# Mixture of experts in two blocks: an eighth home for expert matrices where x lies, loads in one piece, and a router that streams rows

## The reference

```python
# block one
x = x + diff_attention(rmsnorm(x), ...)            # 8 heads, two softmaxes each, causal
xt = rmsnorm(x, norm_ffn)                          # 512 x 1024
logit_g = xt @ w_group + b_group                   # 4 groups
logit_e = xt @ w_router + b_router                 # 4 experts in each
g = argmax(logit_g); two best experts e of group g, with weights w
y[n] = sum over the 2 experts of w * (silu(xt @ w_gate[e]) * (xt @ w_up[e])) @ w_down[e]
x = x + y
# block two
n = rmsnorm(x) * (1 + scale) + shift
p = n @ w_in                                       # Fourier input and gate, q, k, v, gate
x = x + gate * (concat(fourier(...), neighbourhood_attention(q, k, v, ctx)) @ w_out)
```

## Time and profile before

| | us |
|---|---|
| median of three timed runs | 907.3 (907.12 to 907.95) |
| the profiled execution | 915.63 |
| its span | 913.9 |
| PE busy in the span | 885.8 |
| mean granted TensorE clock | 0.988 of full |

### The profile page before, as it was taken

The page is one execution under the profiler, slowest core; times in us unless marked ns, Lnnn a source line. Parts: engine busy times, 40 slices in busy tenths (PEclk is TensorE's granted clock), DMA queues, the critical chain, the costliest instruction groups (busy, mean ns, idle before and its releaser), DMA issues.

```text
span 913.9 us, 13488 instructions
## 1 busy us (share of the span) xinstructions
PE 885.8 (97%) x5418; PEld 527.4 (58%) x5418; DVE 365.6 (40%) x824; ACT 210.7 (23%) x464; POOL 156.5 (17%) x155
## 2 busy tenths in 40 slices
PE   8999999999999999999898989899999999999998
PEld 5588875456564743345333333344688888856653
DVE  2765442457755473120202010047635542444331
ACT  2211223345543310110000000024202111633320
POOL 3211220000002052050302000033202213260000
PEclk9999999999999799999999999999999999999999
DMA  9945569124012978999999999961382102700002
GB/s 325 319 112 185 185 214 392 63 97 180 1 47 91 184 239 276 358 409 419 413 420 415 419 418 422 403 248 47 111 172 99 48 8 81 241 1 1 1 12 80
DMA packets 79455, 186.38 MB, mean 204 GB/s; under 512 B 32016, under 2 KB 32672, under 8 KB 68512
## 3 DMA queue, kind: packets, MB, share of 16 engines
q1 hardware_dynamic: 71072, 162.41, 49.5%
q0 software_dynamic: 4976, 16.79, 4.9%
q10 hardware_dynamic: 3344, 6.30, 1.8%
HBM read 168.17 MB, written 17.31 MB: 203 GB/s over the span
## 4 chain that ended last, share of the span: by engine, by line
PE 86%; DVE 4%; issue 3%; DMA 2%; ACT 2%; POOL 2%; SPq 0%; DVEq 0%; ACTq 0%; POOLq 0%
PE psum L1029 20%; PE psum L1241 17%; PE psum L1267 8%; PE psum L943 6%; PE psum L1408 5%; PE psum L1131 5%; PE psum L1079 4%; PE psum L1056 4%; PE psum L1093 2%; PE psum L1110 2%; PE psum L1479 2%; PE psum L1369 2%; PE psum L1153 1%; POOL qk_st L2708 1%; PE psum L992 1%
## 5 line engine op out<-in xcount | busy, mean ns | idle before, releaser
L1241 PE MATMUL psum<-ring,buf_a 128*32 128x512 f32 x1232 | 157.9, 597 | 3.1 <-issue 3.0
L1241 PEld LDWEIGHTS psum<-ring,buf_a 128*32 128x32 f32 x1232 | 57.5, 111 | 88.4 <-issue 88.4
L1267 PE MATMUL psum<-ring,buf_c 128*32 128x512 f32 x624 | 82.6, 611 | 11.0 <-issue 11.0
L2415 DVE TENSOR_TENSOR buf_c<-buf_c,psum 128x512 f32<-128x512 f32 x11 | 11.7, 1065 | 190.7 <-PE psum L1241 190.7
L1029 PE MATMUL psum<-ring,buf_a 128*128 128x256 f32 x320 | 70.9, 380 | 0.0
L2785 POOL DMA_INDIRECT buf_b<-xq_d,o_sb x44 | 45.6, 1037 | 147.0 <-DVE buf_a L2388 97.2
L2708 POOL TENSOR_TENSOR qk_st<-qk_st,half 128x8 f32<-128x8 f32 x26 | 43.6, 1676 | 158.6 <-DVE qk_st L2479 72.9
L1029 PEld LDWEIGHTS psum<-ring,buf_a 128*128 128x128 f32 x320 | 60.1, 190 | 8.2 <-issue 0.4
L1029 PE MATMUL psum<-ring,buf_b 128*128 128x256 f32 x288 | 64.8, 380 | 0.0
L1991 DVE TENSOR_TENSOR s_buf<-s_buf,psum 128x512 f32<-128x512 f32 x52 | 35.3, 685 | 61.3 <-PE psum L1029 57.6
L1267 PEld LDWEIGHTS psum<-ring,buf_c 128*32 128x32 f32 x624 | 28.0, 112 | 53.9 <-issue 53.9
(11 more groups left out here) (350 smaller groups left out, 1265.3 us busy)
## 6 DMA issues: line engine op xcount, KB each, us to landing
ring<-in_moe_w_gate SPq DMA_DIRECT2D x28, 1024.0 KB, 16.9
ring<-in_moe_w_up SPq DMA_DIRECT2D x28, 1024.0 KB, 15.1
ring<-in_moe_w_down SPq DMA_DIRECT2D x28, 1024.0 KB, 14.1
ring<-in_w_in SPq DMA_DIRECT2D x7, 2048.0 KB, 15.1
ring<-in_w_ada SPq DMA_DIRECT2D x6, 2048.0 KB, 10.3
ring<-in_da_w_in SPq DMA_DIRECT2D x5, 2048.0 KB, 16.1
y_d<-ring POOLq DMA_DIRECT2D x1, 6656.0 KB, 24.8
y_d<-buf_b ACTq DMA_DIRECT2D x10, 512.0 KB, 8.9
```

Of the source, the lines that this page charges most:

```text
L1241: last = mm(buf("mm", n)[rows, :], x_part[:, j, k, :], half_weights(half_load(q, m, r, h)[0], at * F, F), start=(k == 0), stop=(k == KD - 1))
L1267: last = mm(buf("sc", n)[rows, m, :], hidT[:, s % 2, f * P + SUB * j:f * P + SUB * (j + 1)], half_weights(half_load(q, 2, r, h)[0], at * D ...
```

## The change

- **Homes.** There are eight homes of a whole matrix: the tile x (X_HOME), ring slots 4 and 5, the pieces, ring slots 0, 3, 2 and 1. Before it is used as a home, x is stored to a new DRAM tensor x_d (four DMAs of 512 KB), and SP waits for these stores (x_stored). After w_in's k part is issued, x is loaded back in four DMAs, and add_gathered waits for them. Matrices 16 to 44, but for those in the pieces, come as one DMA of 2 MB, after the full pass of the matrix eight before; the first 16 and the last three come in halves.
- **SP's order.** The first eight go 1, 2, 6, 4, 5, then the x stores and quarter stores (x 0 to 2, quarters of tiles 0 and 1, x 3, quarters of tiles 2 and 3), the wait for x_stored, then 0 (into x), 3 (the pieces), 7. The k part of w_in is asked for after the last gate pass.
- **Router.** w_rt (20 columns) stands and xT2 streams: eight calls of 384 columns (tiles 0 to 2), of which six stand before the transposes of the last tile, and eight of 128. ACT copies the 20 x 512 result (logit_T, in pT) and PE turns it back with four small transposes. The first gate row goes between, the second behind.
- **Order around it.** cxT 0 and 1 move into the attention steps 39 and 40; `places` takes the bank that the router's turned result held; cv is cut at 3 and 7 instead of 2 and 6.

The diff, cut to its core:

```diff
@@ attention_steps @@
+    if HEADS * TT + 7 <= s < HEADS * TT + 9:
+        todo.append(("cxT", s - HEADS * TT - 7))
@@ homes @@
-HOMES = [8, 9, 10, 11, 0, 1, 2, 3, 4, 5, 6, 7, 12, 13]
+PIECES, X_HOME = 6, 7
+HOMES = [X_HOME, 4, 5, PIECES, 0, 3, 2, 1]
+def in_halves(i):
+    return i < 2 * len(HOMES) or i >= 45 or HOMES[i % len(HOMES)] == PIECES
...
@@ banks @@
-    for m in range(KD // 2):
+    for m in (2, 3):
         book("tp", "cxT", m)
+    book("mm", "router_T")
+    book("mm", "g_x", 0)
     book("mm", "router")
-    for c in range(2):
-        book("mm", "g_x", c)
+    book("mm", "g_x", 1)
     book("mm", "places")
@@ SP @@
+            if not in_halves(i):
+                sp.dma_start(homes[home].rearrange("p (k n) -> p k n", k=ks), matrix(m, e)).then_inc(landed, 16)
...
+        def store_x(t):
+            sp.wait_ge(xs2_ready, t + 1)
+            sp.dma_start(x_d[t * P:(t + 1) * P, :], x[:, t, :]).then_inc(x_stored, 16)
...
-        for i in [0, 1, 4, 2, 5, 6, 3]:
+        for i in [1, 2, 6, 4, 5, 0, 3, 7]:
...
+            elif i == 0:
+                for t in range(TT - 1):
+                    store_x(t)
+                store_quarters(0)
+                store_quarters(1)
+                store_x(TT - 1)
+                store_quarters(2)
+                store_quarters(3)
+                sp.wait_ge(x_stored, TT * 16)
...
+                if i == 3:
+                    if h == 0:
+                        filled(sp, "mm", turn["mm", "router"])
+                        filled(sp, "tp", turn["tp", "cxT", KD // 2 - 1])
+                    else:
+                        sp.wait_ge(xq_stored, 4 * TT * 16)
...
+            if in_halves(i):
+                for h in range(2):
+                    used(*order[i - len(HOMES)], h)
+                    load_part(q, m, r, h, e)
+            else:
+                used(*order[i - len(HOMES)], 1)
+                load_part(q, m, r, 0, e)
...
+                if c == 0:
+                    filled(sp, "mm", turn["mm", "gate", SETS - 1])
+                elif c == 1:
+                    for t in range(TT):
+                        sp.dma_start(x[:, t, :], x_d[t * P:(t + 1) * P, :]).then_inc(x_loaded[t], 16)
+                    filled(sp, "mm", turn["mm", "up", SETS - 2])
@@ PE @@
+        def router_three(lo, hi):
+            for k in range(lo, hi):
+                drained(pe, "tp", turn["tp", "xT2", k])
+                mm(buf("mm", n_r)[0:20, 0:LAST], w_rt[:, k, :], xT2[:, k, 0:LAST], start=(k == 0), stop=(k == KD - 1))
...
+        router_three(0, 6)
+        pe.wait_ge(xs2_ready, TT)
...
+        router_three(6, KD)
+        for k in range(KD):
+            drained(pe, "tp", turn["tp", "xT2_last", k // 4])
+            last = mm(buf("mm", n_r)[0:20, LAST:SEQ], w_rt[:, k, :], xT2[:, k, LAST:SEQ], start=(k == 0), stop=(k == KD - 1))
+        fill(last, "mm", n_r)
+        pe.wait_ge(gate_ready, 1)
+        gate_row(0)
+        n = turn["mm", "router"]
+        claim(pe, "mm", n)
+        drained(pe, "mm", n_r)
+        for t in range(TT):
+            last = transpose(buf("mm", n)[:, t * 20:(t + 1) * 20], logit_T[:, t * P:(t + 1) * P], ident[0:20, 0:20])
+        fill(last, "mm", n)
+        gate_row(1)
         cx_transposes(2)
         cx_transposes(3)
-        cv_products(0, 2)
+        cv_products(0, 3)
@@ DVE @@
                 dve.wait_ge(yg_ready[(2 * t + c) % 4], 16 * ((2 * t + c) // 4 + 1))
+                if c == 0:
+                    dve.wait_ge(x_loaded[t], 32)
```

More of the change, by code:

```diff
@@ L208, in moe_load, with landings @@
     return 12 + 9 * (q - 1) + 3 * m + r
-def half_load(q, m, r, h):
-    n = 2 * moe_load(q, m, r) + h
-    return HOMES[n % len(HOMES)], n // len(HOMES) + 1
+def in_halves(i):
+    return i < 2 * len(HOMES) or i >= 45 or HOMES[i % len(HOMES)] == PIECES
+def landings(q, m, r, h):
+    i = moe_load(q, m, r)
+    home, each = HOMES[i % len(HOMES)], 2 if HOMES[i % len(HOMES)] == PIECES else 1
+    others = range(i % len(HOMES), i + 1, len(HOMES))
+    if h == 0:
+        return 16 * (LANDED_FIRST[home] + each * len(others))
+    return 16 * each * sum(in_halves(j) for j in others)
 def pass_at(m, s):
@@ L633, in build @@
     w_landed = [sem(f"w_landed{i}") for i in range(SLOTS)]
-    home_landed = [sem(f"home_landed{i}") for i in range(len(HOMES))]
+    w_landed += [sem("pieces_landed"), sem("x_home_landed")]
+    second_landed = [sem(f"second_landed{i}") for i in range(len(HOMES))]
+    x_stored = sem("x_stored")
     half_pass = sem("half_pass")
@@ L944, in transposes, with cx_transposes @@
             fill(last, "tp", n)
+        def cx_transposes(m):
+            n = turn["tp", "cxT", m]
+            claim(pe, "tp", n)
+            transposes(n, [cx[:, t, k * P:(k + 1) * P] for k in (2 * m, 2 * m + 1) for t in range(CT)])
         def h_transposes(t):
@@ L1628, in _, with cx_copies @@
         S.activation(lam[:, 2:4], lam[:, 0:2], ACT.Exp).then_inc(lam_exp, 1)
+        def cx_copies(m):
+            n = turn["tp", "cxT", m]
+            filled(act, "tp", n)
+            for kk in range(2):
+                k = 2 * m + kk
+                last = S.activation(cxT[:, k, :], buf("tp", n)[:, kk * CTX:(kk + 1) * CTX], ACT.Identity,
+                                    bias=mod_sh[:, 1, k:k + 1], scale=mod_g[:, 1, k:k + 1])
+            drain(last, "tp", n)
         for s in range(ATTENTION_STEPS):
@@ L1676, in _, with gate_row_copy @@
         drain(S.copy(xT2[:, 0:4, LAST:SEQ], buf("tp", n).rearrange("p (k n) -> p k n", k=4)), "tp", n)
-        def cx_copies(m):
-            n = turn["tp", "cxT", m]
-            filled(act, "tp", n)
-            for kk in range(2):
-                k = 2 * m + kk
-                last = S.activation(cxT[:, k, :], buf("tp", n)[:, kk * CTX:(kk + 1) * CTX], ACT.Identity,
-                                    bias=mod_sh[:, 1, k:k + 1], scale=mod_g[:, 1, k:k + 1])
-            drain(last, "tp", n)
-        act.wait_ge(mod_ready, 1)
-        cx_copies(0)
-        cx_copies(1)
+        n = turn["mm", "router_T"]
+        filled(act, "mm", n)
+        drain(S.copy(logit_T, buf("mm", n)[0:20, :]), "mm", n)
+        def gate_row_copy(c):
+            n = turn["mm", "g_x", c]
+            filled(act, "mm", n)
+            drain(S.copy(g_x[:, c * 512:(c + 1) * 512], buf("mm", n)), "mm", n)
+        gate_row_copy(0)
         act.wait_ge(ge_in, 1)
@@ L1693, in _ @@
         S.activation(in_group[:], in_group[:], ACT.Exp).then_inc(ge_out, 1)
+        gate_row_copy(1)
         cx_copies(2)
         cx_copies(3)
-        for c in range(2):
-            n = turn["mm", "g_x", c]
-            filled(act, "mm", n)
-            drain(S.copy(g_x[:, c * 512:(c + 1) * 512], buf("mm", n)), "mm", n)
         n = turn["sc", "cv"]
```

156 lines of the change are left out of this document (74 added, 82 removed).

## The result

The changed kernel takes 911.48 us (median of five, 909.73 to 911.96) against 907.3 (906.44 to 908.37): ratio 1.0041, 95% interval 1.0026 to 1.0055. It is slower by 4.2 us where 1.9 less was forecast, a hair outside the range given (900.2 to 911.4) and inside what rival C was priced at (909.9 to 912.4). All comparisons are between fast runs; three executions of 3249 to 5236 us, one each of the kernel before and of experiments 8 and 10, are left out.

The account below looks back on a forecast made before the run. TensorE is busy nearly throughout, and the weight stream was taken to end the mixture-of-experts stage in timed runs. Terms -4.5 - 0.3 + 2.1 + 0.8 = -1.9 us gave 905.4 timed; its own range 903.5 to 906.8, overall 900.2 to 911.4.

Parts of the forecast that it names:

- rival C: Slower: weights don't bind in timed runs, relief is 0, the stage's start pays; 909.9 to 912.4, say 910.8; chance 0.32.
- start of the gathers: Mixture of experts' start: stores in at 326.3, later than indices at 324.4, so gathers start 0.3 us earlier.
- gathers beside loads: Gathers land later because 4.2 MB queue up just then; 0 to +3.7 us, taken as +2.1.
- idle and clock: PE idles from 331.5 to 336.5 before the first pass, then partly lower clock: 0 to +1.66, taken as +0.8.
- weights: Eighth home takes 5.0 us off the full weight stream, counting only as far as weights bind: -4.5 us.
- end of the stage: Reload of x behind k's w_in, in a queue that is full anyway, costs 0; at worst +1 us.
- What bounds the kernel: PE busy nearly all the span; in timed runs the stream of weights sets the mixture-of-experts stage's end.
- The 8.3 us: Profiled execution's excess over the timed median, put wholly into the mixture-of-experts stage, so timed passes outrun their weights by 4.5.
- unexplained stalls of 12.4 us: PE's excess over 3 x 42.8 us in the first three trios, called "issue"; the reason for placing the 8.3 us there.
- Stores of x: Stores of x before and between the quarter stores: 2.10 MB, 5.0 us, so quarters are in at about 326.3.
- Router and indices: Streaming x through the router fills its bank 0.9 us earlier, places 1.3 more; indices at 324.4 instead of 326.65.
- Whole loads: Loads starting only when both halves of the old matrix are read: 0; up to 3.4 us with an empty queue.

Follow-up runs that it names:

- experiment 8: Kernel of experiment 4 (matrix 7 in x, stores of x last) with every matrix loaded in two halves: 904.99 us, ratio 0.9973.
- experiment 10: The change's router on the kernel before, with seven homes, no store of x, and quarter stores moved early: 903.63 us, ratio 0.9960.
- before's second profile: Second profile of the unedited kernel before, taken in experiment 1: 905.62 us, where the first profile took 915.63.
- experiment 1: The kernel before once more, no edit, for a second profile: 906.46 us, ratio 0.9998.
- experiment 7: Kernel of experiment 4, with SP holding back loads and stores of x until the first four gathers have landed: 911.26 us, ratio 1.0045.
- experiment 5: The change's router with the kernel before's seven homes and halves; x stored and loaded back, nothing put in its place: 915.7 us, ratio 1.0103.
- experiment 6: The change, with the four stores of x behind the 16 quarter stores instead of ahead and between: 906.71 us, ratio 0.9993.
- experiment 9: The change, with stores of x and quarters moved early, those of tiles 0 to 2 before the waits for w_out: 902.1 us, ratio 0.9953.
- experiment 2: The kernel before with only the change's router part (edits of PE, ACT and banks, none of SP): 904.76 us, ratio 0.9972.
- experiment 4: The change, with x as home of matrix 7 instead of 0, and stores of x behind the quarters and pieces: 905.81 us, ratio 0.9991.
- experiment 3: The change without its router, cxT and cv edits, leaving only the homes and SP's order: 909.02 us, ratio 1.0023.
- the first profile of before: The profile of the kernel before that the prediction rested on: 915.63 us, 8.3 above the median of its timed runs.

## Why the prediction was wrong, step by step

The terms, forecast and as the two profiles have them (change against before's second profile; both from 903.9 and 909.9 us of span):

| step | forecast | measured | from |
|---|---|---|---|
| start of the gathers | -0.3 | +2.9 | 329.22 - 326.34 |
| gathers beside loads | +2.1 | +3.2 | (340.50 - 329.22) - (334.46 - 326.34) |
| idle and clock | +0.8 | +2.4 | 16.31 - 13.87 |
| weights | -4.5 | -3.9 | first pass to the last `down` but one's end, 241.6 - 2.4 against 243.0 |
| end of the stage | 0 | +1.4 | 327.8 against 326.4 us from there to the end |
| sum | -1.9 | +6.0 | span +6.0, timed +4.2 |

Every term missed on the same side, by 3.2, 1.1, 1.6, 0.6 and 1.4 us in the order of the table. The first is the largest.

- *What bounds the kernel* was right, by a doubtful road. That the stream of weights sets the end in the usual runs, though the profile in hand showed 3.8 us of slack, held (0.2 us of slack in experiment 1; experiments 7 and 10). The size, -4.5, was near (-3.9; -4.2 between experiment 5 and the change), which is part luck. The 8.3 us do lie in this stage, but not in the "unexplained stalls of 12.4 us" of the trios that the choice rested on: of these, 6.9 (0.72 + 1.58 in each of three trios) are in every profile, so that a trio's ideal is 45.09 us and not 42.8, and 9.8 of the 11.5 us between the two profiles of before lie ahead of the trios. Rival C's condition, no weights bind, did not hold. C's time was reached by other means.
- *Stores of x* is the step that failed. The prediction said "2.10 MB at 418 is 5.0 us, so the quarters are in at about 321.3 + 5.0 = 326.3 if everything stands in line". They were in at 328.37, 2.1 us later; the first gather left 0.8 us after that, where the term had nothing, and 0.3 is the difference between the two profiles of before (326.65 and 326.34). So the start came 2.9 us later instead of 0.3 earlier, and the stores, not the indices (ready near 323.7), set it by over 5 us. The x stores themselves moved at about the rate assumed (408 and 389 GB/s in 309 to 311 and 311 to 313 us). Behind them the quarter pieces moved at 150 and 130 GB/s from 323 to 327 us, where the kernel before had 172 to 174 from 311 to 321; why is open. The move of these stores alone was worth 4.8 us (experiment 6) and, to before the waits for w_out, 9.4 us (experiment 9). The window that would have told where they cost little stood in the trace of the kernel before (279 to 300.9 us, the DMA engines 0.26 busy, 97 GB/s):

```profile
279.00:300.90 21.90, 20.70 (x73) 10.69 (x72) 10.24 (x18) 6.51 (x12) 4.22 (x7) 1.00 0.26 97
```

- *Router and indices* was right in direction and too small. The granted clock was 1.00 from 301 to 316 us; the indices were ready at about 323.7 (the gathers of experiments 2, 4, 6 and 10 start between 323.62 and 323.85) against a forecast of 324.4. But its worth in the change was below zero: 2.5 us by the medians (experiment 3), of which the clock lost to idle time is shown and the rest not, since the stores decided the start and the earlier end of cv became idle time. The prediction had both facts, 5 us of idle and its price, and did not ask what the router's gain does when the gathers are late for another reason.
- *Gathers beside loads*: 6.3 us to land, near the row of 6.86; the term was taken at 2.1 and measured 3.2. The Trainium skill's rule of turns between queues (DMA: Bandwidth & Descriptors, "Queues, rings and completion order"), as the prediction applied it, would have put this term near 0, and the measurement decides.
- *Idle and clock*: 9.5 us of idle, not 5, and the half clock then lasted 2.4 us' worth. The price isn't capped by the one row that the trace had, and it doesn't follow from the idle time alone: the 128 matmuls behind 3.0 us of idle took 13.94 us (experiment 3), behind 4.7 us 15.64 (experiment 6), and behind a wait for weights of 2.2 us in the last trio 15.64 too (experiments 2 and 10), but 13.94 behind one of 2.3 (experiment 1).
- *Whole loads* at 0: right within 0.8 us (experiment 8).
- *The end*: 0 was wrong, +1.4 here. The store of y_d took 7.65 instead of 6.26 us, PE waited 2.24 instead of 0.78 us for the new x, and fell to half clock for it (3.30 instead of 1.88 us for four matmuls). What of it is due to whole loads and what to x's reload in the queue was only compared across kernels (6.82 with halves, 6.78 with the homes alone, which has whole loads too), not settled.

Not settled either: why the first profile of before had stalls of up to 3.4 us called "issue" ahead of a `down`, where the twelve other profiles have at most 1.6, and why its passes ahead of the trios took 9.8 us more.

## What to carry to other kernels

Where loads wait for homes, a stage has two clocks, the passes and the stream, and both start late when its first input is late: price a store or load ahead of the stage by where it stands in the queue, and look first for a stretch ahead in which the DMA engines are idle and the data are already final. A step that makes an engine ready earlier is worth nothing, or less, until what it then waits for is earlier too; idle time of TensorE costs its length and can then cost the clock. Price a new home net of the traffic that it brings: here 6.5 us of relief left 1.5. And don't build a sum on the stalls or the slack of a single profiled execution that is 1% above the timed median.

## What was not expected of the hardware

- The clock: with 20 streamed columns in each of 40 matmuls in a row the granted clock was 0.53 over 305 to 316 us, with PE busy all the time (kernel before, second profile); in the change, where 20 columns of weights stand and 384 and 128 columns stream, it was 1.00 over the same stretch.
- Moving 3.6 MB less over 28 us was followed by 6.9 us of waits on `up` weights, in three waits of up to 3.4 (experiment 7; none in experiment 8).
- Stores of 128-byte pieces hold their issuer: eight of them kept SP 13.63 us in the change (queued behind 3.7 MB), and four kept it 3.46 us with little more than one 512 KB store ahead of them (experiment 9).
